# Two transformer blocks on one core: modulation sums stacked by rows, and the second half of a feed-forward's norm behind part 1's gate scaling

## The chip, the cores and the metric

The kernel runs on one core of a Trainium2 chip. A core has five engines: TensorE (PE) multiplies matrices, VectorE (DVE) and ScalarE (ACT) work element by element, GpSimd (POOL) does side work, and SyncE (SP) here only issues DMA transfers. Each engine works its own list in order and waits for semaphores that others count up. The metric is the device time of one execution in microseconds (us).

## The reference, cut to what matters

Two programs run one after the other in one kernel, each on a sequence of 256 positions with 1024 channels, in fp32. The first has two layers (mixer, then a feed-forward with a causal convolution of three taps on the gate):

```
h = rmsnorm(x, ffn_norm_g)
g = causal_dwconv(h @ w_gate, conv_w) + conv_b
x = x + (silu(g) * (h @ w_up)) @ w_down
```

The second has two layers of feed-forward, mixer (pooling and latent attention), feed-forward, each with a modulated norm and a gated residual:

```
mod = silu(c) @ ada_w[l] + ada_b[l]              # 1024 -> 9 x 1024, for l = 0, 1
(sh1, sc1, g1, sh2, sc2, g2, sh3, sc3, g3) = split(mod, 9)
h = rms_norm(x, norm) * (1 + sc) + sh
x = x + 0.5 * g * swiglu(h, w_gate, w_up, w_down)
```

`mod` does not depend on `x`: its 18 vectors of 1024 (72 MB of weights) are computed beside the rest.

## The kernel before, in words

**Stages.** ev (first mixer), ffn0, od (second mixer), ffn1, then for l = 0 and 1: fa (feed-forward), w (mixer), fb (feed-forward). The sequence lies in the free dimension, channels on the partitions.

**Weights.** SyncE loads units of 1 MB into a ring of three (`raw`, L461). ScalarE rounds each to fp32r (`hi`, L1070, the copy is L1078), VectorE subtracts to get the remainder (`lo`, L1501, L1507), and TensorE multiplies high and low parts. `split_done` counts the finished units, `w_used` those that TensorE is through with.

**A feed-forward** has 11 parts of 256 hidden channels, with a gate, an up and a down unit each. TensorE (`ffn`, L752) does gate and up of parts 0 and 1 on the input before the norm's scale is known (`raw_unit`, L619, L635 and L644), then the down unit of part 0, and then `block(j)` for j = 2 to 10: gate and up of part j (L666, L667, on the normalised input `HP`) and the down unit (L768) of part j - 1. The last down unit (L809) waits for part 10's product, written at L1672. For each part ScalarE copies one half of the gate result out of PSUM (L1144), VectorE adds the other (L1632; for parts 0 and 1 it scales instead, L1626), and in ffn0 and ffn1 ScalarE makes the first tap (L1150), VectorE the other two (L1641). Then follow the split of the next gate unit, the up sum (L1654), the product (L1663), and the product's split (L1177, L1672).

**The norm's output** `HP` for parts 2 to 10 is made in two halves, `chain[0]` and `chain[1]`: VectorE scales (L1541), ScalarE rounds (L1111, or L1114 with a shift), VectorE makes the remainder (L1548 or L1552). The second half is made at the end of part 0 (`mid=chain[1]`, L1186 and L1682).

**Modulation.** One step loads 128 rows of `ada_w` by 1024 columns of one vector v, one transfer of 512 KB with one row per partition, into a ring of four (`load_ada`, L477, L482). VectorE multiplies by a column of `CA` (silu(c), one value per partition) and adds into v's own region of `Z` (`ada_step`, L1597: a plain multiply for the first step of a vector, L1603, a multiply-add for the other seven, L1606). Four steps go into each of the parts 2 to 2n + 1, for the n vectors of that feed-forward: ffn0 4, ffn1 3, fa0 4, fb0 3, fa1 4. Then TensorE sums over the partitions (`ada_sum_rows`, L686): for each half of 512 columns, n matmuls with a 128x4 matrix of one column of ones, put at row v (L694). This is done in the stages od, fa0, w0, fa1 and w1. ScalarE copies the rows out (L1098), and TensorE turns them (L702).

**Around it.** In od, TensorE goes from the row sums to small matmuls on `lru_xc` (L941), whose four tiles VectorE makes at L1944 and L1947. In fa0 and fa1 the row sums stand ahead of the first gate unit. In w0 and w1 they stand ahead of the query units, which wait for normalised inputs from L2069. `angles` (L1745: 14 short VectorE instructions for the position tables) stands ahead of part 9 of ffn1. At the start SyncE loads 35 parameter rows with 37 transfers (L517 to L532), which TensorE turns at L882.

Of the kernel before, what the change touches and what calls it, by code (L numbers as in the profile page):

```python
# [51 lines left out]
def param_rows():  # L52
# [13 lines left out]
    r.append(("lam", "od_lru_lam", (0,), 4))  # L66
    r.append(("c", "c_2", (), 8))
    r.append(("qng", "od_q_norm_g", (0,), 1))
# [41 lines left out]
def const_layout():  # L110
    at = 0
    for name, n in (("ident", P), ("ones", P), ("freq", 1), ("eps", 1), ("mask", 3 * P), ("identb", P // 2), ("heads", 22), ("rot", P),
                    ("cmask", 2 * P), ("krdup", P), ("krrot", P), ("pick", 7), ("edge", 4 * 16)):
        CONST[name] = (at, n)
        at += n
    return at
# [7 lines left out]
def constants():  # L124
# [44 lines left out]
    put("freq", np.tile(inv, 4)[:, None])  # L169
    pk = np.zeros((P, 7), np.float32)  # L170
    pk[:, 3] = 1.0
    put("pick", pk)
# [67 lines left out]

ADA_SUMS = {"ffn0": 4, "ffn1": 3, "fa0": 4, "fb0": 3, "fa1": 4}
ADA_GAP = {"od": 4, "fa0": 3, "w0": 4, "fa1": 3, "w1": 4}
AC_AT = {"ffn0": 0, "ffn1": 0, "fa0": 1536, "fb0": 0, "fa1": 1536}
# [7 lines left out]

N_PAR = len(param_rows()) + 2
TWO_PI = 6.283185307179586
# [14 lines left out]
def build(nc, A, const, out):  # L268

    ctx = ExitStack()  # L270
    with ctx:
# [31 lines left out]
        HG = sb("HG", [P, 4, KD])  # L303
        CA = sb("CA", [P, KD])
        SM = sb("SM", [P, 48])
# [9 lines left out]
        def bank(i, a=0, n=512, rows=slice(0, P)):  # L315
            return PS[rows, i, a:a + n]
# [139 lines left out]
        def _(sp):  # L456
# [17 lines left out]

            aw = A["ada_w_2"].rearrange("l (k p) n -> p l k n", p=P)

            def load_ada(step):  # L477
                g, k = divmod(step, KD)
                if step >= ADA_RING:
                    sp.wait_ge(ada_sum, step - ADA_RING + 1)  # L480
                l, v = divmod(g, N_ADA // 2)
                sp.dma_start(ada[:, step % ADA_RING], aw[:, l, k, v * D:(v + 1) * D]).then_inc(ada_in[step % ADA_RING], 16)  # L482

            def load_ffn(name, gate, up, down):
# [10 lines left out]
                def ada_part(j, *ks):  # L495
                    if name in ADA_AT and 2 <= j <= 2 * ADA_SUMS[name] + 1:
                        for k in ks:
                            load_ada(KD * ADA_AT[name] + 4 * (j - 2) + k)

# [17 lines left out]
            for i, (name, src, index, rows) in enumerate(param_rows()):  # L517
                if i in (10, 24):
                    early = i > 10
                    load_in(U0["ev_in"] + 3 + early, w, EV_ORDER[3 + early:4 + early], 2560)  # L520
                g, r = divmod(PCOL[name], P)
                v = A[src]
                for at in index:
                    v = v[at]
                dst = AR[r:r + rows, g * P:(g + 1) * P]
                if name in ("qng", "kng"):
                    for h in range(2):
                        sp.dma_start(dst[:, 64 * h:64 * h + 64], v.unsqueeze(0)).then_inc(par_in, 16)
# [86 lines left out]
        def _(pe):  # L615
# [446 lines left out]
        def _(act):  # L1062
# [68 lines left out]
            def ffn(f, chain):  # L1131
                n0, fb, conv = U0[FFNS[f]], f * NFB, f < 2

                def part(j, par, ng, nu, nd, off=0, mid=None):
# [43 lines left out]
                    if late:  # L1178
                        hi(nu + 3, off)
                    if mid is not None:  # L1180
                        mid()
# [108 lines left out]
            act.wait_ge(ev("par_out"), NPG)  # L1290
            A_(CA[:], pc("c", 0, 8), ACT.Silu).then_inc(ev("silu_c"), 1)
            act.wait_ge(ev("ln_normed"), 1)
# [204 lines left out]
        def _(dve):  # L1497
# [98 lines left out]

            def ada_step(at, at_z, off, k):  # L1597

                step = KD * at + k
                dve.wait_ge(ada_in[k % ADA_RING], 16 * (step // ADA_RING + 1) + 16 * (KD // ADA_RING) * off)  # L1600
                total, w = Z[:, bass.ds(off * D + at_z, D)], ada[:, k % ADA_RING]
                if k == 0:
                    ins = ts(total, w, CA[:, 0:1], None, ALU.mult)  # L1603
                else:
                    dve.wait_ge(ada_sum, KD * off + step)
                    ins = stt(total, w, CA[:, k:k + 1], total, ALU.mult, ALU.add)  # L1606
                ins.then_inc(ada_sum, 1)

            def ffn(f, name, gain, gate=None, chain=None, at_end=None):
# [4 lines left out]
                def part(j, par, ng, nu, nd, off=0, ks=(), mid=None):  # L1614
                    def ada_some(i):
                        for k in ks[i]:
                            ada_step(ADA_AT[FFNS[f]], AC_AT[FFNS[f]], off, k)

# [5 lines left out]
                    if start:  # L1624
                        dve.wait_ge(w_used, ng + 1)
                        ins = tt(pairs(E if conv else C), PS[:, 4:6, 0:S], over(RS[:, 0:S], 2), ALU.mult)  # L1626
                        if not conv:
                            ins = dve.tensor_reduce(BI[:, 4 * j:4 * j + 2], PS[:, 4:6, S:RW], AX.X, ALU.add)  # L1628
                        ins.then_inc(g_sum, 1)
                    else:  # L1630
                        dve.wait_ge(g_copy, j + fc)
# [41 lines left out]
                    if late:  # L1673
                        lo(nu + 3, off)
                    if mid is not None:
                        mid()
                    if nd is not None:
# [3 lines left out]
                chain[0]()  # L1681
                part(0, 0, n0, n0 + 1, None, mid=chain[1])  # L1682
                part(1, 1, n0 + 2, n0 + 3, n0 + 4)
                steps = [((4 * b,), (4 * b + 1,), (4 * b + 2, 4 * b + 3)) if sums else () for b in range(2)]
                n = sums or 3
                with dve.Fori(0, n) as i:
# [490 lines left out]
```

## Time and profile before

| | |
|---|---|
| median of 3 executions | 1613.81 us (1613.39 to 1614.95) |
| profiled execution | 1613.69 us |
| its span, first to last instruction | 1611.7 us |
| TensorE busy | 1589.0 us (99%) |
| VectorE busy | 1262.0 us (78%) |
| ScalarE busy | 855.1 us (53%) |
| mean busy share of the DMA engines by stretch of 40 us | 0.17 to 0.96 |

TensorE's time is made of matmul records; an fp32 matmul leaves two of them. They overlap in part, so the distance from start to start is what counts. Durations of VectorE and ScalarE also overlap by some 0.08 us with the next instruction.

### The profile page before, as it was taken

To read this page: it belongs to the slowest core of one execution; us is meant where nothing else is said; L and a number is where in the kernel's file an instruction comes from. 1 tells how busy PE (TensorE), PEld (TensorE's weight loads), DVE (VectorE), ACT (ScalarE), POOL (GpSimd) and SP (SyncE) were. 2 spreads that over 40 slices of the span, in tenths; PEclk is the share of its full clock that TensorE was granted. 3 is DMA by queue.
4 is the path that set the end of the run, shared out by engine and by line. 5 is a ranking of instruction groups with operands and counts; after the bars stand their busy time and mean duration, and the time that the engine had idled before them with its cause. 6 is when DMAs were issued, how large, how long until landed. Compare 5 with 4: busy or idle time off the path is not lost.

```text
span 1611.7 us, 26970 instructions
## 1 busy us (share of the span) xinstructions
PE 1589.0 (99%) x11042; PEld 1451.2 (90%) x11044; DVE 1262.0 (78%) x1447; ACT 855.1 (53%) x1025; POOL 58.6 (4%) x76
## 2 busy tenths in 40 slices
PE   9999999999999999999999999999999999999998
PEld 8989999988898999899998899999899998899997
DVE  7978889877678997878878697885878887785555
ACT  6566555555465545644446474445544455564443
POOL 3001000000010000000000010000000000010000
PEclk9999999999999999999999999999999999999999
DMA  9414988644238885498864349875598854265552
GB/s 266 162 53 161 349 300 304 217 158 147 79 119 299 299 290 180 146 325 310 314 216 135 112 158 329 314 243 183 173 324 301 308 167 160 93 196 183 185 194 76
DMA packets 231438, 343.48 MB, mean 213 GB/s; under 512 B 7066, under 2 KB 194048, under 8 KB 231360
## 3 DMA queue, kind: packets, MB, share of 16 engines
q1 hardware_dynamic: 230304, 340.94, 62.4%
q0 software_dynamic: 752, 1.18, 0.2%
q8 instruction: 55, 0.90, 0.2%
q10 hardware_dynamic: 304, 0.27, 0.1%
q14 instruction: 23, 0.19, 0.0%
HBM read 341.32 MB, written 1.05 MB: 212 GB/s over the span
## 4 chain that ended last, share of the span: by engine, by line
PE 80%; DVE 10%; issue 6%; ACT 3%; DMA 0%; DVEq 0%; ACTq 0%
PE PS L666 21%; PE PS L768 19%; PE PS L667 11%; PE PS L657 9%; PE PS L635 5%; PE PS L738 3%; DVE wl L1507 3%; PE PS L644 3%; PE PS L694 2%; PE PS L905 2%; ACT wh L1078 1%; DVE XL L1523 1%; DVE Z L1606 1%; PE PS L832 1%; PE PS L854 1%
## 5 line engine op out<-in xcount | busy, mean ns | idle before, releaser
L1507 DVE TENSOR_TENSOR wl<-raw,wh 128x2048 fp32r<-128x2048 f32 (+2 forms) x256 | 570.1, 2229 | 147.3 <-ACT wh L1078 145.3
L666 PE MATMUL PS<-HP,wh 128*128 128x512 f32 x1728 | 608.0, 395 | 2.1 <-DVE wl L1507 2.1
L1078 ACT ACTIVATE wh<-raw 128x2048 fp32r<-128x2048 f32 (+2 forms) x256 | 475.5, 1859 | 134.0 <-PE PS L768 114.9
L667 PE MATMUL PS<-HP,wl 128*128 128x256 f32 x1728 | 484.6, 280 | 0.0
L666 PEld LDWEIGHTS PS<-HP,wh 128*128 128x128 f32 x1728 | 324.0, 188 | 76.7 <-DVE wl L1507 2.5
L768 PE MATMUL PS<-FX,wh 128*128 128x256 f32 x1920 | 345.0, 281 | 0.4 <-DVE FX L1672 0.4
L667 PEld LDWEIGHTS PS<-HP,wl 128*128 128x128 f32 x1728 | 326.5, 189 | 0.0
L768 PEld LDWEIGHTS PS<-FX,wh 128*128 128x128 f32 x1920 | 294.5, 188 | 2.9 <-issue 0.6
L768 PE MATMUL PS<-FX,wl 128*128 128x256 f32 x960 | 269.9, 281 | 0.0
L768 PEld LDWEIGHTS PS<-FX,wl 128*128 128x128 f32 x960 | 180.4, 188 | 0.0
L1606 DVE SCALAR_TENSOR_TENSOR Z<-ada,CA,Z 128x1024 f32 x126 | 161.4, 1281 | 1.3
L635 PE MATMUL PS<-FX,wh 128*128 128x258 f32 (+2 forms) x592 | 145.0, 285 | 4.7 <-DVE BI L1628 1.8
L635 PE MATMUL PS<-FX,wl 128*128 128x258 f32 (+2 forms) x592 | 143.7, 282 | 0.0
L657 PE MATMUL PS<-HP,wh 128*128 128x256 f32 x768 | 140.9, 285 | 1.2 <-ACT HP L1111 0.6
L1144 ACT ACTIVATE WK<-PS 128x512 f32<-128x512 f32 x54 | 32.3, 598 | 196.8 <-PE PS L667 196.8
L657 PEld LDWEIGHTS PS<-HP,wh 128*128 128x128 f32 x768 | 119.8, 192 | 7.3 <-issue 2.6
L635 PEld LDWEIGHTS PS<-FX,wh 128*128 128x128 f32 (+1 forms) x592 | 111.1, 188 | 8.7 <-DVE BI L1628 2.2
L635 PEld LDWEIGHTS PS<-FX,wl 128*128 128x128 f32 (+1 forms) x592 | 111.2, 188 | 0.0
L657 PE MATMUL PS<-HP,wl 128*128 128x256 f32 x384 | 107.5, 283 | 0.0
L1169 ACT ACTIVATE WK<-PS 128x512 f32<-128x512 f32 x54 | 32.0, 593 | 97.1 <-PE PS L667 97.1
L644 PE MATMUL PS<-XL,wh 128*128 128x256 f32 (+1 forms) x592 | 77.5, 282 | 0.0
L657 PEld LDWEIGHTS PS<-HP,wl 128*128 128x128 f32 x384 | 73.6, 192 | 0.0
(286 smaller groups left out, 1752.7 us busy)
## 6 DMA issues: line engine op xcount, KB each, us to landing
ada<-ada_w SPq DMA_DIRECT2D x144, 512.0 KB, 6.0
raw<-ffn_w_gate SPq DMA_DIRECT2D x66, 1024.0 KB, 5.4
raw<-ffn_w_up SPq DMA_DIRECT2D x66, 1024.0 KB, 5.4
raw<-ffn_w_down SPq DMA_DIRECT2D x66, 1024.0 KB, 5.0
raw<-od_w_in SPq DMA_DIRECT2D x13, 1024.0 KB, 5.3
raw<-ev_w_in SPq DMA_DIRECT2D x10, 1024.0 KB, 8.1
raw<-w_in SPq DMA_DIRECT2D x8, 1024.0 KB, 5.4
raw<-w_out SPq DMA_DIRECT2D x8, 1024.0 KB, 5.8
```

The lines of the kernel that those rows point to most:

```text
L635: mm(bank(dst + m, 0, width, slice(0, rows[m])), lhsT=w(a, k, m * P, rows[m]), rhs=XH[:, k, 0:width], start=k == 0 and a == 0, stop=False, ...
L644: last = mm(bank(dst + m, 0, S, slice(0, rows[m])), lhsT=w(0, k, m * P, rows[m]), rhs=XL[:, k, :], start=False, stop=k == KD - 1, skip_gro ...
L657: last = mm(dst, lhsT=lhs(a, k), rhs=rhs(b, k), start=first and i == 0, stop=first and i == len(order) - 1, skip_group_check=not first)
L666: mm(pairs(bank(bk)), lhsT=lhs(0, k), rhs=HP[:, k], start=k == 0, stop=False, skip_group_check=True)
L667: last = mm(bank(bk, 0, S), lhsT=lhs(1, k), rhs=HH[:, k, :], start=False, stop=k == k_tiles - 1, skip_group_check=True)
L694: last = mm(bank(bk + h, 0, 512, slice(0, 4)), lhsT=cn("pick")[:, 3 - v:7 - v], rhs=Z[:, at + v * D + 512 * h:at + v * D + 512 * h + 512], ...
L738: last = mm(bank(bk, m * S, S), lhsT=w(a, k, m * P, P), rhs=H[b][:, k, :], start=m == 0 and k == 0 and i == 0, stop=False, skip_group_chec ...
L768: last = mm(bank(m // 2, (m % 2) * S, S), lhsT=w(a, k, m * P, P), rhs=rhs(b, k), start=begins and i == 0 and m % 2 == 0, stop=False, skip_ ...
L1078: last = A_(dst(wh), src, ACT.Copy)
L1144: A_(pairs(E), PS[:, 4:6, S:], ACT.Copy).then_inc(g_copy, 1)
L1507: last = tt(dst(wl), src, dst(wh).bitcast(F32), ALU.subtract)
L1606: ins = stt(total, w, CA[:, k:k + 1], total, ALU.mult, ALU.add)
```

## The change

1. `part(1)` gets `mid=chain[1]` in the place of `part(0)`. On VectorE `mid` now stands behind the gate scaling of the part (L1626), ahead of the taps; on ScalarE behind the first tap, ahead of the split of the next gate unit.
2. The n vectors of a feed-forward are stacked over the partitions: one step holds, in four groups of 32 partitions, 32 rows of each of four vectors (or 64 rows of each of two). A step is loaded with four transfers of 32 partitions. All steps of a feed-forward add into one region of `Z` of 1024 columns, which VectorE clears first; the plain multiply is gone. `ada_sum_rows` is one matmul per half, with a matrix that sums each group into its row. `CA` holds silu(c) in both layouts, from two parameter rows (`c4`, `c2`) loaded with six transfers instead of one; the parameters then fill six groups of columns instead of five.
3. The counts become 4, 4, 4, 4, 2 for ffn0, ffn1, fa0, fb0, fa1 (before: 4, 3, 4, 3, 4), 144 steps in all as before. So ffn1 and fb0 have steps in the parts 2 to 9 and fa1 in the parts 2 to 5.
4. `angles` moves from ahead of part 9 to ahead of part 10 of ffn1, the only part behind its loop.

```diff
-ADA_SUMS = {"ffn0": 4, "ffn1": 3, "fa0": 4, "fb0": 3, "fa1": 4}
+ADA_SUMS = {"ffn0": 4, "ffn1": 4, "fa0": 4, "fb0": 4, "fa1": 2}
...
-            def load_ada(step):
-                g, k = divmod(step, KD)
+            def load_ada(step, at, n):
                 if step >= ADA_RING:
-                    sp.wait_ge(ada_sum, step - ADA_RING + 1)
-                l, v = divmod(g, N_ADA // 2)
-                sp.dma_start(ada[:, step % ADA_RING], aw[:, l, k, v * D:(v + 1) * D]).then_inc(ada_in[step % ADA_RING], 16)
+                    sp.wait_ge(ada_sum, step - ADA_RING + 2)
+                for i in range(4):
+                    l, v = divmod(at + i * n // 4, N_ADA // 2)
+                    r = (step - KD * at) * (P // n) + (0 if n == 4 else 32 * (i % 2))
+                    sp.dma_start(ada[32 * i:32 * i + 32, step % ADA_RING],
+                                 aw[l, r:r + 32, v * D:(v + 1) * D]).then_inc(ada_in[step % ADA_RING], 16)
...
                 for h in range(2):
-                    for v in range(n):
-                        last = mm(bank(bk + h, 0, 512, slice(0, 4)), lhsT=cn("pick")[:, 3 - v:7 - v],
-                                  rhs=Z[:, at + v * D + 512 * h:at + v * D + 512 * h + 512], start=v == 0, stop=v == n - 1)
+                    last = mm(bank(bk + h, 0, 512, slice(0, 4)), lhsT=pick, rhs=Z[:, at + 512 * h:at + 512 * h + 512],
+                              start=True, stop=True)
...
                         last.then_inc(g_first, 1)
+                    if mid is not None:
+                        mid()
                     hi(ng + 3, off)
...
-                part(0, 0, n0, n0 + 1, None, mid=chain[1])
-                part(1, 1, n0 + 2, n0 + 3, n0 + 4)
+                part(0, 0, n0, n0 + 1, None)
+                part(1, 1, n0 + 2, n0 + 3, n0 + 4, mid=chain[1])
...
-                total, w = Z[:, bass.ds(off * D + at_z, D)], ada[:, k % ADA_RING]
-                if k == 0:
-                    ins = ts(total, w, CA[:, 0:1], None, ALU.mult)
-                else:
-                    dve.wait_ge(ada_sum, KD * off + step)
-                    ins = stt(total, w, CA[:, k:k + 1], total, ALU.mult, ALU.add)
-                ins.then_inc(ada_sum, 1)
+                total, w = Z[:, at_z:at_z + D], ada[:, k % ADA_RING]
+                dve.wait_ge(ada_sum, KD * off + step + 1)
+                c = CA[:, bass.ds(KD * off + (0 if n == 4 else 32) + k, 1)]
+                stt(total, w, c, total, ALU.mult, ALU.add).then_inc(ada_sum, 1)
...
+                if sums:
+                    zero = dve.memset(Z[:, AC_AT[FFNS[f]]:AC_AT[FFNS[f]] + D], 0.0)
...
-                    if f == 1 and j == 9:
+                    if f == 1 and j == 10:
                         angles()
```

## Rows read from the trace of the kernel before

**Rows 1.** The page of the whole span: busy time, share of span, instructions of each engine.
```profile
PE 1589.0 (99%) x11042; PEld 1451.2 (90%) x11044; DVE 1262.0 (78%) x1447; ACT 855.1 (53%) x1025; POOL 58.6 (4%) x76
```

**Rows 2.** Timeline of TensorE around od's row sums: start, duration (us), engine, line.
```profile
344.26 7.03 PE L694 MATMUL PS<-Z,CN 128*4 128x512 f32 x16
...
351.23 0.70 PE L941 MATMUL PS<-T,PW 128*128 128x256 f32 x2
```

**Rows 3.** Timeline of VectorE at the convolution of od.
```profile
348.83 3.25 DVE L1947 SCALAR_TENSOR_TENSOR T<-Z,PR,T 128x256 f32<-128x256 f32 x8
```

**Rows 4.** Timeline of VectorE in w0, ahead of and behind the query units.
```profile
882.45 1.49 DVE L2069 TENSOR_TENSOR HP<-Z,HP 128x1280 fp32r<-128x1280 f32 x1 [1.34 <-ACT HP L1430]
...
893.26 2.29 DVE L1507 TENSOR_TENSOR wl<-raw,wh 128x2048 fp32r<-128x2048 f32 x1 [2.82 <-ACT wh L1078]
```

**Rows 5.** Timeline of VectorE, then of TensorE, at the start of ffn0.
```profile
150.14 1.67 DVE L1541 SCALAR_TENSOR_TENSOR T<-X,PR,RS 128x256 f32<-128x256 f32 x4
...
155.04 1.67 DVE L1641 SCALAR_TENSOR_TENSOR WK<-WK,PR 128x255 f32<-128x255 f32 x4 [1.25 <-ACT WK L1150]
...
156.85 2.29 DVE L1507 TENSOR_TENSOR wl<-raw,wh 128x2048 fp32r<-128x2048 f32 x1
...
159.20 0.50 PE L666 MATMUL PS<-HP,wh 128*128 128x512 f32 x1 [1.06 <-DVE wl L1507]
```

**Rows 6.** Timeline of VectorE, then ScalarE (gate copies, first and last of 9), ffn0.
```profile
183.24 0.68 DVE L1632 TENSOR_TENSOR WK<-PS,WK 128x512 f32<-128x512 f32 x1
...
200.63 0.68 DVE L1632 TENSOR_TENSOR WK<-PS,WK 128x512 f32<-128x512 f32 x1
...
217.48 0.68 DVE L1632 TENSOR_TENSOR WK<-PS,WK 128x512 f32<-128x512 f32 x1
...
329.59 0.27 DVE L1923 MEMSET RS<- 128x256 f32 x1
...
165.23 0.60 ACT L1144 ACTIVATE WK<-PS 128x512 f32<-128x512 f32 x1 [2.21 <-PE PS L667]
...
300.42 0.60 ACT L1144 ACTIVATE WK<-PS 128x512 f32<-128x512 f32 x1 [3.23 <-PE PS L667]
```

**Rows 7.** Timeline of VectorE, then of TensorE, in the last part of ffn0.
```profile
303.35 0.68 DVE L1632 TENSOR_TENSOR WK<-PS,WK 128x512 f32<-128x512 f32 x1
...
312.24 0.47 PE L768 MATMUL PS<-FX,wh 128*128 128x256 f32 x2 [0.44 <-DVE FX L1672]
```

**Rows 8.** Timeline of VectorE in ffn1: part 2, angles, parts 9 and 10.
```profile
500.34 0.69 DVE L1632 TENSOR_TENSOR WK<-PS,WK 128x512 f32<-128x512 f32 x1 [0.33 <-ACT WK L1144]
...
616.66 0.28 DVE L1749 CAST WK<-SIN 128x256 f32<-128x256 int32 x1
...
621.39 0.69 DVE L1632 TENSOR_TENSOR WK<-PS,WK 128x512 f32<-128x512 f32 x1
...
635.53 0.69 DVE L1632 TENSOR_TENSOR WK<-PS,WK 128x512 f32<-128x512 f32 x1 [1.58 <-ACT WK L1144]
```

**Rows 9.** Busy by stretch: us, PE, PEld, DVE, ACT, POOL, clock, DMA, GB/s; then DMA landings.
```profile
160.00:200.00 40.00, 40.00 (x261) 36.39 (x260) 35.94 (x34) 21.11 (x21) 0.00 (x0) 1.00 0.96 341
...
1040.00:1080.00 40.00, 40.00 (x261) 36.35 (x260) 33.49 (x27) 18.43 (x17) 0.00 (x0) 1.00 0.82 282
...
ada<-ada_w SPq DMA_DIRECT2D x144, 512.0 KB, 6.0
```

**Rows 10.** Timeline of SyncE, ScalarE and TensorE at the parameters.
```profile
25.70 0.25 SPq L532 DMA_DIRECT2D AR<-kv_a_norm  x1
...
29.90 1.92 ACT L1078 ACTIVATE wh<-raw 128x2048 fp32r<-128x2048 f32 x1 [1.52 <-DMA raw<-ev_w_in]
...
32.27 0.68 PE L882 MATMUL PS<-CN,AR 128*128 128x128 f32 x5
```

**Rows 11.** Busy by stretch at the end of the span, columns as in rows 9.
```profile
1605.00:1612.00 7.00, 0.33 (x4) 0.09 (x1) 2.94 (x8) 3.23 (x10) 0.00 (x0) 0.68 0.40 150
...
1607.50:1611.70 4.20, 0.00 (x0) 0.00 (x0) 0.55 (x1) 0.79 (x2) 0.00 (x0) 0.50 0.67 250
```

More of the change, by code:

```diff
@@ L66, in param_rows @@
     r.append(("lam", "od_lru_lam", (0,), 4))
-    r.append(("c", "c_2", (), 8))
+    r.append(("c4", "c_2", (), 32))
+    r.append(("c2", "c_2", (), 16))
     r.append(("qng", "od_q_norm_g", (0,), 1))
@@ L169, in constants @@
     put("freq", np.tile(inv, 4)[:, None])
-    pk = np.zeros((P, 7), np.float32)
-    pk[:, 3] = 1.0
+    pk = np.zeros((P, 8), np.float32)
+    for i in range(P):
+        pk[i, i // 32] = pk[i, 4 + i // 64] = 1.0
     put("pick", pk)
@@ L238 @@
     _n += SUM_PARTS.get(_name, 3)
-ADA_SUMS = {"ffn0": 4, "ffn1": 3, "fa0": 4, "fb0": 3, "fa1": 4}
-ADA_GAP = {"od": 4, "fa0": 3, "w0": 4, "fa1": 3, "w1": 4}
+ADA_SUMS = {"ffn0": 4, "ffn1": 4, "fa0": 4, "fb0": 4, "fa1": 2}
+ADA_GAP = {"od": 4, "fa0": 4, "w0": 4, "fa1": 4, "w1": 2}
 AC_AT = {"ffn0": 0, "ffn1": 0, "fa0": 1536, "fb0": 0, "fa1": 1536}
@@ L250 @@
 assert _a == N_ADA
-N_PAR = len(param_rows()) + 2
+COPIES = {"qng": 2, "kng": 2, "c4": 4, "c2": 2}
+N_PAR = sum(COPIES.get(e[0], 1) for e in param_rows())
 TWO_PI = 6.283185307179586
@@ L303, in build @@
         HG = sb("HG", [P, 4, KD])
-        CA = sb("CA", [P, KD])
+        CA = sb("CA", [P, 48])
         SM = sb("SM", [P, 48])
@@ L525, in _ @@
                 dst = AR[r:r + rows, g * P:(g + 1) * P]
-                if name in ("qng", "kng"):
-                    for h in range(2):
-                        sp.dma_start(dst[:, 64 * h:64 * h + 64], v.unsqueeze(0)).then_inc(par_in, 16)
+                if name in COPIES:
+                    m = P // COPIES[name]
+                    for h in range(COPIES[name]):
+                        sp.dma_start(dst[:, m * h:m * h + m], v.rearrange("(t p) -> t p", p=m)).then_inc(par_in, 16)
                     continue
@@ L1179, in part @@
                         hi(nu + 3, off)
-                    if mid is not None:
-                        mid()
                     if nd is not None:
@@ L1595, in out_units, with ada_step @@
                 raw_lo(name, 2, gain)
-            def ada_step(at, at_z, off, k):
+            def ada_step(name, off, k):
+                at, at_z, n = ADA_AT[name], AC_AT[name], ADA_SUMS[name]
                 step = KD * at + k
-                dve.wait_ge(ada_in[k % ADA_RING], 16 * (step // ADA_RING + 1) + 16 * (KD // ADA_RING) * off)
-                total, w = Z[:, bass.ds(off * D + at_z, D)], ada[:, k % ADA_RING]
-                if k == 0:
-                    ins = ts(total, w, CA[:, 0:1], None, ALU.mult)
-                else:
-                    dve.wait_ge(ada_sum, KD * off + step)
-                    ins = stt(total, w, CA[:, k:k + 1], total, ALU.mult, ALU.add)
-                ins.then_inc(ada_sum, 1)
+                dve.wait_ge(ada_in[k % ADA_RING], 64 * (step // ADA_RING + 1) + 64 * (KD // ADA_RING) * off)
+                total, w = Z[:, at_z:at_z + D], ada[:, k % ADA_RING]
+                dve.wait_ge(ada_sum, KD * off + step + 1)
+                c = CA[:, bass.ds(KD * off + (0 if n == 4 else 32) + k, 1)]
+                stt(total, w, c, total, ALU.mult, ALU.add).then_inc(ada_sum, 1)
             def ffn(f, name, gain, gate=None, chain=None, at_end=None):
@@ L1616, in ada_some @@
                         for k in ks[i]:
-                            ada_step(ADA_AT[FFNS[f]], AC_AT[FFNS[f]], off, k)
+                            ada_step(FFNS[f], off, k)
                     ks = ks or ((), (), ())
@@ L1629, in part @@
                         ins.then_inc(g_sum, 1)
+                        if mid is not None:
+                            mid()
                     else:
@@ L1681, in ffn @@
                 chain[0]()
-                part(0, 0, n0, n0 + 1, None, mid=chain[1])
-                part(1, 1, n0 + 2, n0 + 3, n0 + 4)
+                part(0, 0, n0, n0 + 1, None)
+                part(1, 1, n0 + 2, n0 + 3, n0 + 4, mid=chain[1])
                 steps = [((4 * b,), (4 * b + 1,), (4 * b + 2, 4 * b + 3)) if sums else () for b in range(2)]
                 n = sums or 3
+                if sums:
+                    zero = dve.memset(Z[:, AC_AT[FFNS[f]]:AC_AT[FFNS[f]] + D], 0.0)
+                    if f == 0:
+                        zero.then_inc(ada_sum, 1)
+                    else:
+                        own.link(zero)
                 with dve.Fori(0, n) as i:
```

16 lines of the change are left out of this document (8 added, 8 removed).

## The prediction

> **What bounds the kernel now.** I read the page first: TensorE is busy 1589.0 us of a span of 1611.7 us [rows 1], at full granted clock, so only 22.7 us of its time are idle. A cut in TensorE's own work moves the end; what is taken off another engine moves it only where TensorE waits. TensorE's waits are short (the longest is 1.06 us [rows 5]), so the question for each piece is: does TensorE's saved time turn into a wait for something that was hidden? The timelines of VectorE, ScalarE and SyncE around each piece answer that.
>
> The change has four parts, though its title names one: the norm's second half moves; the modulation sums (`ada`) are laid out anew; with that, two feed-forwards get more of these steps and one fewer; and two parameter rows replace one.
>
> **1. Summing the modulation rows on TensorE.** `ada_sum_rows` issues 2 matmuls instead of 2 x 4 or 2 x 3. Each fp32 matmul shows as two records; 16 records take 6.97 us from their start to the next line's [rows 2], 0.436 us each; the 12 at fa0 and fa1 so take 5.2 us, and four take 1.74. Nominally that is 5.2 us saved at od, w0 and w1 and 3.5 us at fa0 and fa1 (22.7 us in all). Place by place:
> - od: the next matmul needs the first tile of the convolution `lru_xc`. VectorE makes the last eight of those instructions from 348.83 us, 0.406 us each [rows 3]; the first tile is the fifth, at 350.9. TensorE would be there at 346.0 and idles 4.9 us. Gain 0.3 us of 5.2.
> - fa0 and fa1: next comes the first gate unit, whose inputs ScalarE has made before TensorE reaches them, and the statistic behind it waits for TensorE. Gain 3.5 us each.
> - w0 and w1: next is the query unit, which waits for the normalised queries. VectorE's instruction for them ends at 883.94 (882.45 + 1.49) [rows 4]; TensorE would be there at 882.0 and waits 1.9. Of the 3.3 us left, the position products pass 2.9 on: VectorE works its list without a gap once the weight split behind the 2.8 us idle in rows 4 comes earlier. Gain 2.9 us each.
> Sum: 0.3 + 3.5 + 3.5 + 2.9 + 2.9 = **13.1 us gained**; bounds 0 and 22.7.
>
> **2. The norm's second half.** In ffn0 VectorE makes it from 150.14, before part 1's gate scaling. Its taps then wait 1.25 us for ScalarE's first tap, and the split of unit n0+5 starts at 156.85; TensorE waits 1.06 us for it [rows 5]. Behind the scaling, ScalarE's first tap runs beside the norm, so the wait goes; ScalarE's two copies for the norm then follow its tap. I get the split at 155.6, 1.25 us earlier, and TensorE's 1.1 us disappears in ffn0 and ffn1. In the four gated feed-forwards ScalarE's split of n0+5 comes behind the norm's activations, some 0.8 us later, and VectorE's split with it; TensorE is then still at the down projection: nothing. Bounds for the four: 0 and 0.8 us each. These gains count only until VectorE is late at the feed-forward's other end (next).
>
> **3. VectorE in ffn0 and ffn1.** One part with four `ada` steps, all of them multiply-adds, takes VectorE 17.39 us (183.24 to 200.63); with one plain multiply in it, 16.85 [rows 6]. TensorE's part takes (300.42 - 165.23) / 8 = 16.90 us [rows 6]. VectorE is the slower one already, and its lag is carried by buffers. The change makes every step a multiply-add, so all parts take 17.39, and adds a clearing of 128x1024. A clearing of 128x256 took 0.27 us [rows 6] for a quarter of the elements, so I take 0.9 us (part of a short instruction is fixed cost), bounds 0.3 and 1.1. VectorE reaches part 2 at 165.06 (0.8 earlier), then needs 8 x 17.39 + 0.1 = 139.2 us to part 10: 304.3 against 303.35 before. The last down projection starts 8.89 us behind that point (312.24 - 303.35) and already waited 0.44 us for it [rows 7]. ffn0 so ends **0.9 us later**, TensorE idling 2.5 us.
> ffn1 had three rounds of sums, now four, and `angles` moves from ahead of part 9 to ahead of part 10. Before, parts 8 and 9 without sums gave room for `angles` (616.66 to 621.39, 4.73 us), and VectorE idled 1.58 us ahead of part 10 [rows 8]. Now: part 2 at 500.34 - 0.7 = 499.6; plus 139.2 is 638.8; plus 4.73 is 643.6, against 635.53. The down projection starts 8.9 us behind, at 652.5. Before it started when TensorE was free: 11.38 us behind the gate copy, as in ffn0 (312.24 - 0.44 - 300.42). That copy takes 0.6 us and its end started the sum at 635.53, so it began at 634.9 and the projection at 646.3. ffn1 ends **6.2 us later**, and TensorE idles 7.3 us. fa0's start loses 0.4 us more, since ScalarE and VectorE are late there. fb0 gets a fourth round and fa1 two; VectorE is busy 33.5 of 40 us in such a stretch [rows 9], so neither shows.
>
> **4. Loads.** An `ada` step comes in four transfers of 32 partitions, 576 in all. They land in 6.0 us in the median [rows 9] and are asked for a part ahead. SyncE issues a transfer in some 0.3 us [rows 10], so four cost it 1.2 us per step and 5 us per part of 17, much of it while it would wait anyway. DMA is 0.96 busy in the first sums of ffn0 [rows 9]. I cost this at nothing: the same bytes, asked for as early as before. At the start, `c4` and `c2` need 6 transfers instead of 1, at 0.34 us from issue to issue: up to 1.75 us. The last parameter is issued at 25.70, TensorE turns them at 32.27 with no idle time, and ScalarE waited until 29.90 for a load that had been issued among the parameters [rows 10]. So they come just in time. I take **1.2 us later**, bounds 0 and 1.75. TensorE's next units follow one another without a wait that could absorb it. A sixth group of parameters costs 0.2 us, under other work.
>
> **5. TensorE's clock.** It was granted in full up to 1607.5 us. TensorE did its last 0.33 us of work just after 1605.0, and from 1607.5 on the clock stood at 0.50, 1.2 of 2.4 GHz [rows 11]. So some idle time costs clock, and the new gaps of 4.9 (od) and 7.3 us (ffn1) are of that size. Work at half clock takes twice as long. I take 1.1 and 1.6 us, **2.7 us** in sum; bounds 0 and 8, if every gap costs what a run of 4 us at half clock loses (2 us). The Trainium skill, "TensorE: Matmul & The Clock Gate", Part 1, says the throttled state is the default and activity releases it; by that, the cost is paid after each long gap. The rows agree as far as they go.
>
> **Sum.** -13.1 + 0.9 + 6.2 + 0.4 + 1.2 + 2.7 = -1.7 us. The profiled execution took 1613.69 us (span 1611.7), 0.1 under the median 1613.81, so **1612.0 us**. A measurement here can tell about 0.2%, 3.2 us, from no change: my forecast is no change.
>
> **Rivals.**
> - The clock holds, or the parameters come in time: -13.1 + 7.5 + 0 to 1.2 gives 1608 to 1609.5. For: no row shows how much idle time the clock bears. Chance 0.25.
> - VectorE's lag in ffn1 is carried by more than I see, and the row sums give what they can: -13.1 - 2.2 + 1.2 gives 1599.6. Against: 17.39 us repeats in every pair, and 0.44 us of wait is there already. Chance 0.07.
> - Slower, by the clock: it falls at all five new gaps (od, ffn0, ffn1, w0, w1) and each costs 2 us: -4.4 + 10 gives 1619.3. It decides as soon as gaps of 2 to 2.5 us suffice; against it, gaps of 1.1 us cost nothing before. Chance 0.2.
> - Slower, by the loads: quarters of 32 partitions run at half rate. `ada` is two of the five MB of a part; 0.96 busy would become over 1.3, and each part with sums 3.5 us longer: 36 such parts, 1738 us. The Trainium skill, "DMA: Bandwidth & Descriptors", Rules for kernel authors, asks for 128 partitions and at least 1 MiB per DMA for the highest bandwidth. No row shows a large transfer of few partitions. Chance 0.04.
> - The change does not do what its title says: the moved half frees nothing lasting. That is in my forecast, and changes no sum.
>
> **How the numbers follow.** Forecast 0.44 (1610 to 1615), the rivals as given. Faster by over 0.2% (under 1610.6): 0.25 + 0.07 and little of the forecast, 0.33; slower (over 1617): 0.24 and a bit, 0.26; the rest 0.41. Range 1606.5 to 1619.5: from both early costs absent to the clock falling at every gap.
>
> **What would show it.** The row-sum line with 20 records instead of 72; TensorE idle some 5 us ahead of the first `lru_xc` matmul, 1.9 us at the query units, some 7 us ahead of ffn1's last down projection and 2.5 at ffn0's, none at n0+5; VectorE's gate sums 17.39 us apart in ffn0; granted clock below 1 in the stretches behind the long gaps. I am wrong if ffn1 ends without a wait, or if ScalarE waits for weights in the parts with sums.

## The result and the profile after

The changed kernel took 1738.67 us in the median of 4 runs (1725.90 to 1747.38), the kernel before 1614.26 beside it: ratio 1.0765, 95% interval 1.0694 to 1.0835. It is **slower by 124 us**. The forecast was 1612.0, the range 1606.5 to 1619.5, with 0.26 on slower; the rival that priced the loads at 1738 us had a chance of 0.04. In the runs below, the chip was in a slower state in one execution each of e2, e3, e6 and e8 (1748.81, 4009.29, 1750.72 and 1927.04 us), and the medians of e2 and e6 over their other executions are 1727.98 and 1725.45 us.

The page of the profiled execution (1735.3 us): the whole span, then, by 40 slices, the granted clock, the share of DMA (in tenths) and its rate; then the chain that ended last.
```profile
span 1733.4 us, 27468 instructions
...
PE 1612.4 (93%) x10991; PEld 1475.1 (85%) x10993; DVE 1274.4 (74%) x1453; ACT 853.4 (49%) x1026; POOL 58.1 (3%) x76
...
PEclk9999999999999899899999999999999999999999
DMA  8526999844249999489995538999779953545552
GB/s 259 164 73 187 259 258 253 226 153 140 71 146 244 247 247 250 152 233 264 257 249 169 163 125 221 241 238 241 199 218 266 254 184 117 164 149 188 181 193 85
...
PE 43%; DMA 25%; DVE 14%; SPq 7%; ACT 6%; issue 5%; DVEq 0%; ACTq 0%
```
TensorE was 99% busy [rows 1] and is now 93%: it idles 121 us where it idled 22.7. A quarter of the chain is DMA.

The same page, the groups that answer for it, and the landing times of the loads:
```profile
L1085 ACT ACTIVATE wh<-raw 128x2048 fp32r<-128x2048 f32 (+2 forms) x256 | 475.6, 1860 | 383.9 <-DMA raw<-ffn_w_down 134.8
...
ada<-ada_w SPq DMA_DIRECT2D x576, 128.0 KB, 9.8
raw<-ffn_w_gate SPq DMA_DIRECT2D x66, 1024.0 KB, 10.9
raw<-ffn_w_up SPq DMA_DIRECT2D x66, 1024.0 KB, 9.7
raw<-ffn_w_down SPq DMA_DIRECT2D x66, 1024.0 KB, 13.5
```
An `ada` step landed in 6.0 us [rows 9], a quarter of one now takes 9.8 us in the median. The weights, which the change doesn't touch, take 9.7 to 13.5 us, where a run below with whole transfers has 5.0 to 5.5. ScalarE, first to take a weight unit, waits for them. Who waits for whom on ScalarE (us in total, times, longest):
```profile
ACT wh L1085 <- DMA raw<-ffn_w_down: 134.8, 33, 5.4
ACT wh L1085 <- DMA raw<-ffn_w_up: 95.1, 31, 4.0
...
ACT wh L1085 <- DMA raw<-ffn_w_gate: 80.9, 17, 6.4
```
And ffn0 by stretches of 40 us, columns as in rows 9; the first answers to the first of rows 9:
```profile
160.00:200.00 40.00, 40.00 (x261) 36.35 (x260) 33.18 (x32) 18.46 (x19) 0.00 (x0) 1.00 1.05 268
200.00:240.00 40.00, 33.92 (x213) 30.20 (x212) 29.54 (x28) 17.69 (x18) 0.00 (x0) 0.96 1.07 259
240.00:280.00 40.00, 37.07 (x224) 33.18 (x224) 30.65 (x31) 17.70 (x18) 0.00 (x0) 0.91 1.07 253
```
The share of the DMA engines was 0.96 and they moved 341 GB/s [rows 9]; now it is 1.05 and they move 268. (The share adds up the times of the packets; where it is over 1.0, these overlap on an engine.) They are busier and move less: each packet takes longer. Over all packet records that start between 210 and 310 us, the mean of one of 4096 bytes (rows of `ada_w` and of the down units) went from 167 to 261 ns, of one of 1024 bytes (for the most part of gate and up units) from 52 to 70. The first stretch loses nothing on TensorE, because it lives on weights loaded ahead; from 200 us on TensorE idles.

Two pieces of the chain in that stretch, start, duration, what, each ahead of one of the waits:
```profile
211.43 14.76 DMA ada<-ada_w
...
248.14 14.32 DMA raw<-ffn_w_down
```

### The profile page after: what moved, and what is told of

The parts are those of the page before. It is cut to its first block, busy times and chain, and to the rows that moved or that the text cites. A ratio compares the mean times of both kernels' runs of the same rounds, so it can differ in the third digit from the quotient of the medians.

```text
span 1733.4 us, 27468 instructions
## 1 busy us (share of the span) xinstructions
PE 1612.4 (93%) x10991; PEld 1475.1 (85%) x10993; DVE 1274.4 (74%) x1453; ACT 853.4 (49%) x1026; POOL 58.1 (3%) x76
## 3 DMA queue, kind: packets, MB, share of 16 engines
HBM read 341.34 MB, written 1.05 MB: 198 GB/s over the span
## 4 chain that ended last, share of the span: by engine, by line
PE 43%; DMA 25%; DVE 14%; SPq 7%; ACT 6%; issue 5%; DVEq 0%; ACTq 0%
DMA raw<-ffn_w_gate 13%; PE PS L775 9%; PE PS L664 7%; PE PS L673 7%; SPq L487 6%; DMA ada<-ada_w 6%; DVE wl L1515 5%; PE PS L642 5%; DMA raw<-ffn_w_down 4%; ACT wh L1085 4%; PE PS L674 4%; PE PS L745 3%; PE PS L651 2%; DMA raw<-ffn_w_up 2%; PE PS L912 1%
## 5 line engine op out<-in xcount | busy, mean ns | idle before, releaser
L673 PE MATMUL PS<-HP,wh 128*128 128x512 f32 x1728 | 632.2, 408 | 55.3 <-DVE wl L1515 55.3
L674 PE MATMUL PS<-HP,wl 128*128 128x256 f32 x1728 | 493.4, 286 | 0.0
L673 PEld LDWEIGHTS PS<-HP,wh 128*128 128x128 f32 x1728 | 334.7, 194 | 141.2 <-DVE wl L1515 51.1
L775 PE MATMUL PS<-FX,wh 128*128 128x256 f32 x1920 | 354.1, 286 | 36.3 <-DVE FX L1680 24.6
L775 PEld LDWEIGHTS PS<-FX,wh 128*128 128x128 f32 x1920 | 301.7, 193 | 44.3 <-issue 30.5
L674 PEld LDWEIGHTS PS<-HP,wl 128*128 128x128 f32 x1728 | 336.6, 195 | 0.0
L1613 DVE SCALAR_TENSOR_TENSOR Z<-ada,CA,Z 128x1024 f32<-128x1024 f32 x144 | 184.3, 1280 | 5.1
L775 PEld LDWEIGHTS PS<-FX,wl 128*128 128x128 f32 x960 | 185.4, 193 | 0.0
L664 PEld LDWEIGHTS PS<-HP,wh 128*128 128x128 f32 x768 | 121.9, 195 | 10.7 <-issue 8.1
L664 PE MATMUL PS<-HP,wl 128*128 128x256 f32 x384 | 108.6, 286 | 0.0
L664 PEld LDWEIGHTS PS<-HP,wl 128*128 128x128 f32 x384 | 74.7, 195 | 0.0
L651 PEld LDWEIGHTS PS<-XL,wh 128*128 128x128 f32 (+1 forms) x592 | 72.9, 186 | 0.5
L1157 ACT ACTIVATE WK<-WK,PR 128x256 f32<-128x256 f32 x44 | 24.1, 594 | 98.3 <-DVE WK L1640 89.4
## 6 DMA issues: line engine op xcount, KB each, us to landing
raw<-ffn_w_down SPq DMA_DIRECT2D x66, 1024.0 KB, 13.5
```

Source lines behind the costliest of these rows:

```text
L651: last = mm(bank(dst + m, 0, S, slice(0, rows[m])), lhsT=w(0, k, m * P, rows[m]), rhs=XL[:, k, :], start=False, stop=k == KD - 1, skip_gro ...
L664: last = mm(dst, lhsT=lhs(a, k), rhs=rhs(b, k), start=first and i == 0, stop=first and i == len(order) - 1, skip_group_check=not first)
L673: mm(pairs(bank(bk)), lhsT=lhs(0, k), rhs=HP[:, k], start=k == 0, stop=False, skip_group_check=True)
L674: last = mm(bank(bk, 0, S), lhsT=lhs(1, k), rhs=HH[:, k, :], start=False, stop=k == k_tiles - 1, skip_group_check=True)
L775: last = mm(bank(m // 2, (m % 2) * S, S), lhsT=w(a, k, m * P, P), rhs=rhs(b, k), start=begins and i == 0 and m % 2 == 0, stop=False, skip_ ...
L1157: last = A_(C[:, m * S:(m + 1) * S], E[:, m * S:(m + 1) * S], ACT.Identity, scale=PR[:, bass.ds(2 * j + c, 1)], bias=PR[:, bass.ds(2 * j + ...
```

## The experiments

Eleven kernels ran. The change lays its loads out in three new ways at once: four transfers a step instead of one, rows of four vectors, 32 partitions each. The first four runs part these.

**e1_whole: the changed kernel, but each step in one transfer.** Its modulation sums combine other rows than the reference's; all times and amounts of work stay.
```diff
-                for i in range(4):
-                    l, v = divmod(at + i * n // 4, N_ADA // 2)
...
+                l, v = divmod(g, N_ADA // 2)
+                sp.dma_start(ada[:, step % ADA_RING],
+                             aw[l, k * P:(k + 1) * P, v * D:(v + 1) * D]).then_inc(ada_in[step % ADA_RING], 16)
```


> The changed kernel, but each modulation step is loaded by one transfer of 128 partitions from the rows of the kernel before. The modulation sums then hold other values, since rows and coefficients no longer match. Theory 'transfers' (the four transfers per step cost the 121 us): about 1612 us, the forecast of the other parts (1606 to 1620), packets of 4096 bytes back to 167 ns in the mean, no wait of ScalarE for weights in the sums, a wait of some 7 us ahead of ffn1's last down projection. Theory 'order' (VectorE's and SyncE's new order is what starves the weights): over 1680 us.

Measured 1616.75 us, ratio 1.0017 (1.0008 to 1.0027). Of the 124 us, 122 come from how the steps are loaded. The rest of the change costs 3 us, and its waits are read below.

**e2_split32: the kernel before, each step in four transfers of 32 neighbouring partitions**, rows as before.
```diff
-                sp.dma_start(ada[:, step % ADA_RING], aw[:, l, k, v * D:(v + 1) * D])...
+                for i in range(4):
+                    sp.dma_start(ada[32 * i:32 * i + 32, step % ADA_RING],
+                                 aw[32 * i:32 * i + 32, l, k, v * D:(v + 1) * D])...
```


> The kernel before; only each modulation load is cut into four transfers of 32 neighbouring partitions, the same rows and bytes. Theories 'narrow' (32 neighbouring partitions are written slowly) and 'count' (four times as many transfers cost) both: 1710 to 1750 us, 4096-byte packets at 260 ns. Theory 'source' (the changed kernel is slow because of the rows it reads, 4 x 32 rows instead of 128): within 5 us of 1614.

Measured 1734.10 us (1718.53 to 1748.81), ratio 1.0716 (1.0638 to 1.0794); packets 263 and 74 ns. The cut alone, in the old kernel, gives nearly the whole loss. So neither the new rows nor anything on VectorE is needed for it.

**e3_columns: the same number of transfers, each of 128 partitions and 256 columns.**
```diff
+                    sp.dma_start(ada[:, step % ADA_RING, 256 * i:256 * i + 256],
+                                 aw[:, l, k, v * D + 256 * i:v * D + 256 * i + 256])...
```


> The kernel before; each modulation load is cut into four transfers of all 128 partitions by 256 columns. Theory 'narrow': within 10 us of 1614, packets of 1024 bytes at about 51 ns. Theory 'count': 1700 us or more, as with the four transfers of 32 partitions.

Measured 1613.94 us, ratio 1.0001 (0.9992 to 1.0011). 576 transfers instead of 144 cost nothing that can be measured.

**e4_step4: the same size and number as e2, but 32 partitions four apart** (0, 4, 8 ... in the first).
```diff
+                    sp.dma_start(ada[i::4, step % ADA_RING], aw[i::4, l, k, v * D:(v + 1) * D])...
```


> The kernel before; each modulation load is cut into four transfers of 32 partitions that lie four apart (0, 4, 8, ...). Theory 'narrow', if what counts is how wide over the partitions one transfer reaches: within 10 us of 1614. Theory 'count', or if what counts is that one transfer has only 32 partitions: 1700 us or more.

Measured 1613.82 us, ratio 0.9999 (0.9989 to 1.0008); packets 173 and 51 ns. This is the telling pair. The stretch from 200 to 240 us of e2, then of e4 (columns as above):
```profile
200.00:240.00 40.00, 33.59 (x211) 30.06 (x210) 28.30 (x30) 17.22 (x18) 0.00 (x0) 0.96 1.07 252
```
```profile
200.00:240.00 40.00, 40.00 (x266) 36.50 (x265) 35.15 (x37) 21.84 (x24) 0.00 (x0) 1.00 0.90 317
```
The bytes and sizes are the same; which 32 of the 128 rows go into one transfer differs: 252 against 317 GB/s. With the partitions the rows of `ada_w` change too, since partition p holds row p of the step: 32 neighbours in memory in e2, every fourth in e4.

**e6_two64 and e8_two_apart: two transfers of 64 partitions**, neighbours in e6, every second one in e8. Is it the number of partitions or their spread?
```diff
+                for i in range(2):
+                    sp.dma_start(ada[64 * i:64 * i + 64, ...], aw[64 * i:64 * i + 64, ...])    # e6
+                    sp.dma_start(ada[i::2, ...], aw[i::2, ...])                                # e8
```


> The kernel before, each ada step loaded by two transfers of 64 neighbouring partitions each; rows, sums and order as before. Theory (a transfer that keeps to neighbouring partitions is slow, by how few partitions it covers): the 4096-byte packets are between the 167 ns of whole transfers and the 263 ns of four quarters, nearer to 200, and the time is above the kernel before by between 0 and 50 us; if it went in proportion to the stretch of the packets, 1640. Rival 1 (only a quarter is slow, half is enough): 1613.7, packets of 4096 bytes at 167 ns. Rival 2 (any cut along neighbouring partitions costs the same): 1730 as with four.

> The kernel before with two transfers for each ada step, of 64 partitions two apart (the even, the odd ones): the control of the run with two halves of 64 neighbours (1726.6). Theory (only the range of partitions that a transfer covers counts, not how many rows it has): 1613.7, 4096-byte packets at 167 to 175 ns. Rival (64 partitions are slow whatever they are): 1726.

Measured: e6 1726.58 us (1714.21 to 1750.72), ratio 1.0748 (1.0686 to 1.0811), packets 264 and 74 ns; e8 1613.97, ratio 0.9999 (0.9990 to 1.0009), packets 176 and 51 ns. I had expected half the cut to do less harm; it does the same. The spread decides, not the count: 64 neighbours are about as bad as 32, and 32 four apart as good as 128. Whether it is the spread over the partitions written or over the rows read, these runs don't show, since both change together.

**e7_half: half the steps as in e6, half as in e8.**
```diff
+                    part = slice(64 * i, 64 * i + 64) if k % 2 else slice(i, P, 2)
```


> The kernel before with two transfers for each ada step: in the odd steps of 64 neighbouring partitions, in the even steps of 64 partitions two apart. It halves the dose of the loads that cover one half of the partitions (112.9 us for all 144 steps). Theory 1 (each such transfer holds up what is under way beside it, so that the loss goes by their number): about half, 1670, between 1650 and 1690, and 4096-byte packets between 167 and 263 ns on average. Theory 2 (the weights of those stages have to land at some rate, and only what goes beyond it costs: of the share of 0.96 that the queue was busy before, there is hardly any room): a little over half. Rival (one of them in any window is enough to spoil the order of the queues): over 1700, as with all of them.

Measured 1648.58 us (1642.91 to 1653.32), ratio 1.0203 (1.0187 to 1.0219): 34.6 us for half the dose, against 112.9 for all. All three forecasts miss; the first two took the loss to be about proportional to the number of slow transfers, and it isn't. The same stretches of e6, then of e7:
```profile
200.00:240.00 40.00, 33.99 (x220) 30.22 (x219) 29.97 (x29) 17.70 (x18) 0.00 (x0) 1.00 1.06 262
240.00:280.00 40.00, 34.40 (x223) 30.59 (x222) 29.67 (x30) 17.70 (x18) 0.00 (x0) 1.00 1.07 250
```
```profile
200.00:240.00 40.00, 40.00 (x265) 36.50 (x264) 33.75 (x33) 18.06 (x18) 0.00 (x0) 1.00 1.06 289
240.00:280.00 40.00, 37.37 (x252) 34.06 (x251) 32.35 (x34) 20.26 (x21) 0.00 (x0) 1.00 1.02 278
```
A part with sums needs 5.24 MB (three weight units and four steps, of 1024 and 512 KB) in 16.9 us: 310 GB/s. An estimate from that: at the 262 GB/s of e6's first stretch it takes 20.0 us, 3.1 more, and times 36 parts 112 us; at the 250 of the second 4.1 more, 147 us; 112.9 was measured. At e7's 289 GB/s it takes 18.1 us, 1.2 more, 43 us in all, at its 278 2.0 more, 71 us; 34.6 was measured. What is loaded ahead carries the first parts of each feed-forward (TensorE has no idle time from 160 to 240 us in e7), so the sum by rates comes out too high; that 262 meets the measured loss is chance. It fits a loss that begins where the rate falls below what a part needs; that a rate a little over 310 would cost nothing is inferred, and no run tested it.

**e5_mid_only: the kernel before with nothing but what the title says**, the second half of the normalised input made in part 1.
```diff
-                part(0, 0, n0, n0 + 1, None, mid=chain[1])
-                part(1, 1, n0 + 2, n0 + 3, n0 + 4)
+                part(0, 0, n0, n0 + 1, None)
+                part(1, 1, n0 + 2, n0 + 3, n0 + 4, mid=chain[1])
```


> The kernel before with one part of the change alone: ScalarE and VectorE make the second half of the normalised input in the second block, ScalarE behind its gate scaling and VectorE behind its gate sum, and no longer at the end of the first block. The prediction's own term: the 1.06 us for which the first matmul of each of the two convolution blocks waits at the last of the early units (rows 5) goes, and this is worth the same at the end of ffn0 and ffn1 only as far as VectorE isn't the last there; so between 1612.4 (one wait gone for good) and 1613.7 (given back at both ends), ratio 0.999 to 1.000. Rival, the move makes the second block late instead: a new wait of TensorE of over 1 us at the gate or up-projection of that block, in ffn0 and ffn1, and the time 1 to 3 us above the kernel before.

Measured 1610.85 us, ratio 0.9983 (0.9974 to 0.9992): 2.9 us faster, more than either theory gave. Timeline of VectorE at the start of ffn0:
```profile
150.88 1.66 DVE L1541 SCALAR_TENSOR_TENSOR T<-X,PR,RS 128x256 f32<-128x256 f32 x4
152.72 1.29 DVE L1548 TENSOR_TENSOR HP<-T,HP 128x512 fp32r<-128x512 f32 x2 [0.18 <-ACT HP L1111]
153.94 1.66 DVE L1643 SCALAR_TENSOR_TENSOR WK<-WK,PR 128x255 f32<-128x255 f32 x4
155.51 2.28 DVE L1507 TENSOR_TENSOR wl<-raw,wh 128x2048 fp32r<-128x2048 f32 x1
```
The 1.25 us ahead of the taps [rows 5] are gone, the split starts at 155.51 (worked out: 155.6) instead of 156.85, and TensorE has no wait at n0+5. From ffn0's end to ffn1's start all comes 1.4 us earlier, from ffn1's end on 2.8, so each gain is kept to the end of its feed-forward: VectorE, too, is 1.34 us earlier from there on.

**f1_interleaved: the changed kernel with spread transfers.** Transfer i fills the partitions i, i + 4, ...; partition 4q + i holds row 32q + t of vector i at step t. The coefficients come straight from `c_2` in that arrangement, `pick` takes partitions modulo 4, and all that is computed is kept.
```diff
-    r.append(("c4", "c_2", (), 32))
-    r.append(("c2", "c_2", (), 16))
...
-        pk[i, i // 32] = pk[i, 4 + i // 64] = 1.0
+        pk[i, i % 4] = pk[i, 4 + i % 4 // 2] = 1.0
...
+                    rows = aw[l].rearrange("(q m) n -> q m n", m=32)[:, t + (0 if n == 4 else 16 * (i % 2)), v * D:(v + 1) * D]
+                    sp.dma_start(ada[i::4, step % ADA_RING], rows)...
...
+                sp.dma_start(CA[i::4, 0:32], A["c_2"].rearrange("(q m) -> q m", m=32))...
```


> The changed kernel, with the four transfers of a step on partitions four apart (0, 4, 8 ... and so on) instead of 32 neighbours: partition 4q+i holds a row of vector i, the coefficients of c are loaded in that arrangement by eight small transfers instead of through the parameter rows, and the one matmul that sums the rows picks by partition modulo 4. All it computes is kept. Theory (neighbouring partitions are the whole excess): TensorE's waits, the clock and the ledger of stages are those of the changed kernel with whole transfers, 1616.7, less up to 1.2 us for the parameter rows that are no longer loaded (1615.5 to 1617.5); packets of 4096 bytes at 167 to 175 ns. Rival (four transfers that bring rows 4096 bytes each from four different vectors are slow by where they read from): over 1650.

Measured 1615.85 us, ratio 1.0012 (1.0003 to 1.0021). The loss of 122 us is gone with the stacking of four vectors kept, and the waits are those of e1. (A transfer's 32 rows now lie 32 apart in `ada_w` as well.)

**f2_angles: f1, with `angles` at part 10 of fa0** instead of part 10 of ffn1, and ScalarE's two sines behind fa0.
```diff
-                    if f == 1 and j == 10:
+                    if f == 2 and j == 10:
                         angles()
```


> The interleaved version of the changed kernel, and the rotary angles (12 VectorE instructions and 2 of ScalarE) made at block 10 of fa0 instead of block 10 of ffn1. Theory (the 7.7 us of TensorE at the last down-projection of ffn1, and the 3.4 us of half clock behind it, come from the angles standing behind the tenth block with row sums): the wait at the end of ffn1 falls to 1 to 3 us and the half clock behind it goes, 5 to 9 us in all; at the end of fa0 VectorE has as much to do as ffn1 had and at_end besides, so that from 0 to 7 us come back there. Between 1607 and 1616; 1610 taken. Rival (the wait just moves to the end of fa0 with all of its price): 1616 to 1618, with a wait of 7 us or more ahead of fa0's last down-projection.

Measured 1611.68 us (1608.99 to 1613.41), ratio 0.9986 (0.9977 to 0.9995). The wait at the last down projection of ffn1 falls from 7.71 to 2.99 us, one of 1.14 us appears at fa0's.

**g1_mixed: f2, with ffn0's sums as in the kernel before**: four vectors apart, first step a plain multiply, no clearing, 16 records of row sums in od. The other feed-forwards keep the interleaved layout.
```diff
+                if at == 0:
+                    total, w = Z[:, bass.ds(off * D + at_z, D)], ada[:, k % ADA_RING]
+                    if k == 0:
+                        ins = ts(total, w, CA[:, 48:49], None, ALU.mult)
...
-                if sums:
+                if sums and f:
```


> The version put together from what the runs showed: row sums of ffn0 as in the kernel before (four vectors apart, the first step a plain multiply, 16 matmuls to sum the rows), those of the other blocks interleaved over the partitions, the second half of the normalised input in the second block, and the angles in fa0. By the ledger: the ends of ffn0 and of od move from 3.4 and 5.1 us later to 1.4 earlier (as the run with the middle move alone has them), so that 6.5 us come off the 1611.68 of the version with the angles in fa0: 1605.2, between 1604 and 1608. Rival (the stretch of half clock at the start of ffn1 or the angles at fa0 take back what ffn0 wins): 1608 to 1612.

Measured 1606.44 us (1606.21 to 1607.17), ratio 0.9955 (0.9942 to 0.9969): 7.5 us faster than the kernel before, the best version. The expected 1605.2 left out that ffn1's wait of 3.00 us stays. TensorE's longest waits in it:
```profile
PE PS L790 <- DVE FX L1705: 4.7, 3, 3.0
PE PS L674 <- DVE HP L2102: 3.7, 2, 1.9
```

## Why the prediction was wrong

**The step that failed is part 4, loads: "I cost this at nothing: the same bytes, asked for as early as before."** The bytes and the time of asking stayed; the rate didn't. Rows 9 gave 0.96 busy at 341 GB/s, so there was next to no room, and the prediction noted it. What was missing was a row with the rate of a transfer to a few neighbouring partitions, and I set the unknown to "as before" instead of to a bound. Its ends should have gone into the range: nothing, and the rival's 1738. The prediction's own sign of being wrong came: ScalarE waits for weights in the parts with sums. The rival ("quarters of 32 partitions run at half rate") had the right place, and its 3.5 us a part stands beside 3.4 measured (122 us over 36 parts). That its size was right is luck, twice. Its 3.5 us doesn't follow from its own step, "0.96 busy would become over 1.3": two of five MB at half rate give 1.34, and 0.34 of 16.9 us is 5.7 us, 207 us in all. And its reason was the number of partitions and the time of these transfers alone; e4 and e6 show that it is the spread, and that the weights beside them slow down too. A chance of 0.04 for a price of 125 us, on a resource at 0.96, was the error. The Trainium skill's rule in "DMA: Bandwidth & Descriptors", Rules for kernel authors (128 partitions and at least 1 MiB per DMA for the highest bandwidth), points in the right direction; e3 with 128 KB transfers (half the 256 KB of e6, and no slower than whole ones of 512 KB) and e4 with 32 partitions break it without loss in this kernel.

**The other terms** are read in e1, where the loads are whole. All of its longer waits of TensorE:
```profile
PE PS L774 <- DVE FX L1679: 10.7, 2, 7.7
PE PS L947 <- DVE T L1958: 4.9, 1, 4.9
PE PS L663 <- DVE HP L2080: 3.7, 2, 1.9
```
- Row sums on TensorE: 20 records instead of 72, and where they pay is as worked out. In od TensorE waits 4.9 us for `lru_xc` (4.9 forecast), at the query units 1.9 us twice (1.9). Against the kernel before, od gives 0.2 us (0.3 forecast), w0 3.1 (2.9) and fa1 3.5 (3.5). w1 gives 1.8 of the 2.9, with a fall of the clock in it. Right but for the clock.
- VectorE in ffn0 and ffn1: right. TensorE idles 3.0 us at ffn0's end and 7.7 at ffn1's (2.5 and 7.3 forecast); the gate sums in ffn0 are 17.48 us apart, at 183.41 and 200.89 (17.39 forecast):
```profile
183.41 0.68 DVE L1639 TENSOR_TENSOR WK<-PS,WK 128x512 f32<-128x512 f32 x1
...
200.89 0.68 DVE L1639 TENSOR_TENSOR WK<-PS,WK 128x512 f32<-128x512 f32 x1
```
- The norm's second half: the wait at n0+5 goes, as forecast. Alone it is worth 2.9 us (e5), 1.4 in each of the two. In the change this is lost in ffn0 and ffn1 to VectorE's later end, as the prediction said.
- Parameters at the start: the first norm's statistic of ffn0 comes 0.9 us later in e1 (1.2 forecast), 0.3 in f1, where `c4` and `c2` aren't parameter rows.
- The clock, forecast 2.7 us, was mis-sized. The granted clock by stretch in e1, where each follows a wait of TensorE (ends of ffn0, od, ffn1; w1's query units); columns as in rows 9:
```profile
314.00:324.00 10.00, 9.27 (x63) 9.10 (x64) 7.92 (x12) 7.96 (x13) 2.21 (x3) 0.83 0.60 191
350.00:360.00 10.00, 6.17 (x32) 5.55 (x33) 7.07 (x10) 2.00 (x5) 0.00 (x0) 0.83 0.61 189
650.00:664.00 14.00, 6.50 (x43) 6.53 (x43) 10.76 (x14) 10.75 (x16) 0.77 (x1) 0.76 0.37 116
1362.00:1372.00 10.00, 8.93 (x62) 8.96 (x63) 8.49 (x11) 5.21 (x6) 0.00 (x0) 0.83 0.32 107
```
A share of 0.83 over 10 us is 3.4 us at the lower level, 1.2 of 2.4 GHz, and half of what TensorE works in that time is lost. In ffn0 and w1 it works all of it, 1.7 us lost each. In od and ffn1 it doesn't; the two stretches at 0.50:
```profile
353.54:356.95 3.41, 3.13 (x8) 2.53 (x9) 3.41 (x5) 0.84 (x2) 0.00 (x0) 0.50 0.81 282
653.91:660.74 6.83, 3.24 (x15) 3.27 (x16) 4.92 (x6) 4.74 (x5) 0.00 (x0) 0.50 0.47 154
```
In ffn1 the clock falls while TensorE still waits (its wait ends at 657.50), so of the 6.8 us only 3.24 are work. The four cost 1.7 + 1.6 + 1.6 + 1.7 = 6.6 us. The timeline of TensorE behind the 3.0 us shows it fall: the same matmul goes from 0.28 to 0.41 us. Then the end of ffn1's wait:
```profile
314.63 0.47 PE L774 MATMUL PS<-FX,wh 128*128 128x256 f32 x2 [2.98 <-DVE FX L1679]
...
315.65 0.28 PE L774 MATMUL PS<-FX,wl 128*128 128x256 f32 x1
...
316.01 0.41 PE L774 MATMUL PS<-FX,wl 128*128 128x256 f32 x1
...
657.50 0.77 PE L774 MATMUL PS<-FX,wh 128*128 128x256 f32 x2 [7.71 <-DVE FX L1679]
```
The forecast had taken only the gaps of 4.9 and 7.3 us to cost clock, 1.1 and 1.6 us (1.6 and 1.6 measured); the falls behind the gaps of 3.0 and 1.9 us it left out.

Put together, the forecast without its failed step was 1612.0 and the run that takes the loads out of the comparison 1616.75. Of the 4.8 us between them 1.9 are the profiled execution of e1 against its own median (1614.86 and 1616.75), which the sum can't hold. The other 2.9 show in how far e1 lags behind the kernel before at the same instructions: 0.9 us at ffn0's first norm, 2.8 at od's row sums (344.26 and 347.06 us), 4.1 at ffn1's first norm, 9.7 behind fa0's row sums, 6.6 behind w0's, 3.2 behind fa1's, 1.4 behind w1's, 1.3 at the end. The forecast's terms give 1.2, 2.1, 2.9, 7.6, 4.7, 1.2, -1.7 and -1.7. The lag outgrows them in ffn0 (by 1.0), od (0.5), ffn1 (0.9) and w1 (1.1), the four stages in which the clock fell, and nowhere else. The clock costs 3.9 us more than forecast; part of it falls where TensorE would have waited anyway, as in ffn0, where the kernel before still waits 0.57 and 0.61 us ahead of od's row sums and e1 doesn't. The rival "slower, by the clock" (1619.3, chance 0.2) described the rest of the change best: the clock fell at four of its five gaps, at 1.6 to 1.7 us instead of 2. Here the profile after is read the wrong way easily: it shows ScalarE waiting for weights and TensorE for ScalarE's and VectorE's units, none of which the change touches. What points at the cause is that the DMA share rose while GB/s fell.

## What to carry to other kernels

Where DMA is near 1.0 busy in the stretch that a change touches, the rate of a new shape of transfer is the first term to bound, not the last; ask what bytes a unit of work needs (here 310 GB/s) and what margin the measured rate leaves (341). If data of several kinds must share the partitions of a tile, interleave them (partition modulo 4, each transfer's rows spread in memory as well, as in f1) instead of giving each a block of neighbours. And a change that bundles a small sound edit with a new layout should be timed apart: the edit of the title alone was worth 2.9 us, while the whole lost 124.

## What the runs showed of the hardware

- Transfers of 32 or 64 neighbouring rows to neighbouring partitions are slow, and the weights' transfers beside them slow down too: packets of 4096 bytes from 167 to 263 ns, the weights' 1024-byte packets from 52 to 74 ns, the rate in ffn0 from 315 (200 to 240 us) to 250 to 262 GB/s. Transfers of as many rows to partitions two or four apart don't do this (173 to 180 and 51 to 53 ns in e4, e8 and f1). What the neighbours share stays open: where the data is written, where it is read (in e2, e6 and the changed kernel the rows of a transfer lie next to each other in `ada_w`, in e4, e8 and f1 they are spread), or which engine serves which partition. The trace doesn't name the DMA engine of a packet, and no run parted the three.
- Cutting a transfer of 512 KB into four of 128 KB over all partitions, 144 times, costs nothing (1613.94 against 1613.66 us).
- In e1 TensorE's clock fell to its lower level at waits of 3.0, 4.9 and 7.7 us (in the last two before the wait was over), and in w1 behind one of 1.86; in w0, behind another of 1.86, it stayed at 1.00. In f2 it was the other way about: it fell behind w0's wait of 1.87 us and not behind w1's. In the same place, the end of ffn1, it stayed up behind a wait of 2.99 us in f2 and fell (0.87 over 13 us) behind one of 3.00 in g1:
```profile
654.00:664.00 10.00, 9.95 (x73) 8.31 (x74) 8.50 (x13) 8.85 (x17) 2.42 (x3) 1.00 0.54 172
```
```profile
647.00:660.00 13.00, 12.59 (x80) 10.95 (x81) 10.86 (x15) 11.13 (x18) 2.27 (x3) 0.87 0.41 135
```
In f1 it fell for 6.8 us at the same wait of 3.0 us that brought 3.4 in e1, with 6.15 us of work in it:
```profile
313.33:320.16 6.83, 6.15 (x29) 6.18 (x30) 4.07 (x5) 4.83 (x5) 0.73 (x1) 0.50 0.58 189
```
So a wait of 2 to 3 us may cost nothing more, or 1.7 to 3.1 us of clock on top: a forecast has to carry both. What decides between them these runs don't show.
